# VectorE's queue in a differential-attention block: products of the next head moved behind the next minimum, and in grouped queries ahead of the exponential

## The reference

```python
def diff(qq, kk, vv, gate):                 # layer 0: 8 heads, 512 + 256 context tokens
    o1 = sweep_attention(qq[..., 0, :], kk[..., 0, :], vv)
    o2 = sweep_attention(qq[..., 1, :], kk[..., 1, :], vv)
    o = o1 - lam.astype(o1.dtype) * o2
    o = rms_norm(o, subln_g) * (1.0 - lam_init)
    return (o.reshape(...) * jax.nn.silu(gate)) @ w_out

q = rms_norm(q.reshape(B, L, GQ_HEADS, GQ_HEAD_DIM), qk_g[0])   # layer 1: 8 query heads, 2 key heads
k = rms_norm(k.reshape(B, L, GQ_KV_HEADS, GQ_HEAD_DIM), qk_g[1])
q, k = apply_rope(q, cos, sin), apply_rope(k, cos, sin)
o = sweep_attention(q, k_all, v_all)
y = (o.reshape(...) * jax.nn.silu(z)) @ w_out
```

## Time and profile before

| | |
|---|---|
| median of 3 runs | 1635.07 us (1634.91 to 1640.42) |
| the profiled execution | 1636.64 us, its span 1635.3 us |
| PE busy | 1533.2 us, 94% of the span |
| DVE, ACT, POOL busy | 69%, 38%, 43% |
| chain that ended last | PE 66%, DVE 15%, ACT 8%, POOL 5% |
| the heads' loops | about 845 to 1290 us, one every 55.0 us |
| grouped queries' 32 steps | about 1405 to 1590 us |

### The profile page before, as it was taken

The page is one execution under the profiler, slowest core; times in us unless marked ns, Lnnn a source line. Parts: engine busy times, 40 slices in busy tenths (PEclk is TensorE's granted clock), DMA queues, the critical chain, the costliest instruction groups (busy, mean ns, idle before and its releaser), DMA issues.

```text
span 1635.3 us, 22570 instructions
## 1 busy us (share of the span) xinstructions
PE 1533.2 (94%) x8093; PEld 1286.4 (79%) x8093; DVE 1133.5 (69%) x2396; ACT 624.7 (38%) x1560; POOL 710.1 (43%) x668
## 2 busy tenths in 40 slices
PE   5998989999999999999999999999997999899997
PEld 4787444788878887877798898889885787899886
DVE  7646766467777768737867777777777588777764
ACT  3313666232222220113453544554455355344431
POOL 6756000337667658685543044314425114523430
PEclk8997999999999999999999999999999999999999
DMA  6623000424444436653320011001102231111221
GB/s 185 196 77 103 1 1 1 140 68 148 129 139 126 129 105 208 203 192 106 122 66 27 26 52 53 26 27 52 53 25 80 107 112 52 53 52 39 65 91 52
DMA packets 115888, 142.62 MB, mean 87 GB/s; under 512 B 11048, under 2 KB 75200, under 8 KB 115776
## 3 DMA queue, kind: packets, MB, share of 16 engines
q1 hardware_dynamic: 89968, 91.77, 18.1%
q10 hardware_dynamic: 25808, 49.40, 9.1%
HBM read 132.74 MB, written 8.40 MB: 86 GB/s over the span
## 4 chain that ended last, share of the span: by engine, by line
PE 66%; DVE 15%; ACT 8%; POOL 5%; issue 4%; DMA 1%; ACTq 0%; SPq 0%; DVEq 0%; POOLq 0%
PE ps L502 17%; PE ps L504 17%; PE ps L503 17%; POOL w_lo L491 3%; PE ps L1445 2%; POOL w_hi L489 2%; PE ps L1249 2%; ACT p L2087 2%; PE ps L908 2%; DVE st L2864 2%; PE ps L889 2%; PE ps L941 1%; DVE p L2536 1%; ACT p L1713 1%; PE ps L1459 1%
## 5 line engine op out<-in xcount | busy, mean ns | idle before, releaser
L489 POOL TENSOR_SCALAR w_hi<-w_raw 128x512 fp32r<-128x512 f32 x308 | 236.1, 767 | 644.8 <-PE ps L504 488.1
L491 POOL TENSOR_TENSOR w_lo<-w_raw,w_hi 128x512 fp32r<-128x512 f32 x316 | 442.4, 1401 | 30.6 <-ACT w_hi L1635 4.9
L502 PE MATMUL ps<-w_hi,h_hi 128*128 128x384 f32 (+2 forms) x768 | 277.1, 361 | 8.2 <-POOL w_lo L491 2.9
L504 PE MATMUL ps<-w_hi,h_lo 128*128 128x384 f32 (+2 forms) x768 | 264.8, 345 | 0.0
L503 PE MATMUL ps<-w_lo,h_hi 128*128 128x384 f32 (+2 forms) x768 | 264.3, 344 | 0.0
L502 PE MATMUL ps<-h_hi,w_hi 128*128 128x512 f32 (+1 forms) x616 | 244.7, 397 | 6.5 <-POOL w_lo L491 2.6
L504 PE MATMUL ps<-h_hi,w_lo 128*128 128x512 f32 (+1 forms) x616 | 237.8, 386 | 0.0
L503 PE MATMUL ps<-h_lo,w_hi 128*128 128x512 f32 (+1 forms) x616 | 237.5, 385 | 0.0
L2582 DVE SCALAR_TENSOR_TENSOR mod_acc<-mod_piece,csil,mod_acc 128x512 f32<-128x512 f32 x140 | 156.7, 1159 | 22.2 <-DMA mod_piece<-in_ada_w 18.3
L502 PEld LDWEIGHTS ps<-w_hi,h_hi 128*128 128x128 f32 x768 | 146.1, 190 | 20.5 <-POOL w_lo L491 4.3
L503 PEld LDWEIGHTS ps<-w_lo,h_hi 128*128 128x128 f32 x768 | 146.5, 191 | 8.4 <-issue 0.5
(11 more groups left out here) (332 smaller groups left out, 3033.6 us busy)
## 6 DMA issues: line engine op xcount, KB each, us to landing
mod_piece<-in_ada_w ACTq DMA_DIRECT2D x96, 256.0 KB, 3.0
w_raw<-in_w_gate_up SPq DMA_DIRECT2D x88, 256.0 KB, 3.1
w_raw<-in_a_w_in SPq DMA_DIRECT2D x128, 128.0 KB, 2.2
w_raw<-in_w_down SPq DMA_DIRECT2D x22, 512.0 KB, 4.2
w_raw<-in_b_w_in SPq DMA_DIRECT2D x20, 512.0 KB, 3.6
w_raw<-in_w_out SPq DMA_DIRECT2D x16, 512.0 KB, 3.8
w_raw<-in_w_in SPq DMA_DIRECT2D x8, 512.0 KB, 3.9
w_raw<-in_w_o SPq DMA_DIRECT2D x8, 512.0 KB, 3.8
```

Of the source, the lines that this page charges most:

```text
L489: pool.tensor_scalar(hi[:, e, :], raw[:, e, :], 1.0, 0.0, ALU.mult, ALU.add).then_inc(*s["pool_step"].up())
L491: m = pool.tensor_tensor(lo[:, e, :], raw[:, e, :], hi[:, e, :], ALU.subtract)
L502: pe.matmul(out, a[0], b[0], start=start, stop=False)
L504: return pe.matmul(out, a[1], b[0], start=False, stop=stop)
```

## The change

In `dve_heads` the read-outs of a step's chunks are no longer issued at the end of that step but in the next step, behind its minimum, the first transposed part and the mix (steps 1 to 11 of heads 0 to 6), and what a loop leaves over (`held`) behind the minimum of the next head's first step. Before, they were issued in part before and in part behind the second L2885 of a step. PE and ACT keep their order there; head 7's own steps keep theirs on DVE too. In `act_grouped` the squares or tanh of a finished unit move from the end of the step to its start, and in `dve_grouped` the unit's rotation or z moves from behind the norm and the second L3092 to between the first L3092 and the norm. No instruction is added or removed.

```diff
@@ act_grouped
     for n in range(32):
+        unit = done_beside8(n)
+        if unit is not None:
+            act_read8(k, act, unit)
         if n > 0:
             act_copy8(k, act, n - 1, 0)
         act_exp8(k, act, n)
         if n > 0:
             act_copy8(k, act, n - 1, 1)
-        unit = done_beside8(n)
-        if unit is not None:
-            act_read8(k, act, unit)
@@ dve_heads
+    held = iter(())
     for hd in range(8):
         beside = dve_beside(k, dve, hd)
...
             if n == 11:
 
                 dve_head_mix(k, dve, hd, 5)
+            if n == 0:
+                for _ in held:
+                    pass
+            elif hd < 7:
+                fill(sum(HEAD_FILL[n - 1]) if n % 2 == 0 else HEAD_FILL[n - 1])
             if n == 3 and hd > 0:
                 dve_head_gate(k, dve, hd - 1)
             if n == 6 and hd > 0:
                 dve_head_y(k, dve, hd - 1)
-            if hd < 7:
-                fill(HEAD_FILL[n][0] if n % 2 else HEAD_FILL[n])
-            elif n in LAST_GATE_READ:
+            if hd == 7 and n in LAST_GATE_READ:
                 fill(KD)
             if late is not None and len(head_turns(late[1])) > 1:
                 dve_head_at(k, dve, *late, 1)
-            if n % 2 and hd < 7:
-                fill(sum(HEAD_FILL[n][1:]))
...
-        for _ in beside:
-            pass
+        held = beside
+    for _ in held:
+        pass
@@ dve_grouped
         if n > 0:
             dve_turned_lo8(k, dve, n - 1, 0)
+        unit = done_beside8(n)
+        if unit is not None:
+            dve_read8(k, dve, unit)
         dve_norm8(k, dve, n)
         if n > 0:
             dve_turned_lo8(k, dve, n - 1, 1)
-        unit = done_beside8(n)
-        if unit is not None:
-            dve_read8(k, dve, unit)
```

## The result

The changed kernel takes 1681.5 us (1679.13 to 1682.51, 4 runs) against 1635.92 for the kernel before on the same chip (1634.91 to 1640.42, 4 runs): 1.0272 times as long, with a 95% interval of 1.0255 to 1.0289. That is 45.6 us slower. The prediction had said 1663 us and a range to 1676: the direction was right, the size was not.

What follows compares the result with a forecast made beforehand. PE was taken as the bound (52.7 of 55 us a head loop). Net +3.5 us over seven loops gave +24, plus 1.5 for grouped queries and 3 for the clock: 1663 us expected, range 1645 to 1676.

Steps and rivals of the forecast that it cites:

- scores' waits of steps 6, 8, 9 go: Head loop: PE's scores no longer wait for ACT's exponential, as the minimum precedes the read-outs; 2.4 us a loop saved.
- POOL's and the transposed part's wait go: Head loop: PE's waits for split weights at chunk 7 (0.71 us) and a transposed part (0.33) were counted as saved.
- chunk 23's turn: Step 4 of a head loop: PE waits for DVE's late turned context tile, 0.8 us added.
- chunk 39's turn: Step 7 of a head loop: PE waits for v and rotation behind minimum and transposed part, 1.3 us added.
- scores of step 10: Head loop: step 9's minimum comes late behind DVE's queued work, so these scores wait about 0.6 us.
- chunk 57: Step 10 of a head loop: PE waits for z1's read-out, 1.4 us added.
- chunk 63's turn: Behind step 11's scores: PE waits for rotation after minimum, transposed part and mix, 2.8 us added.
- the clock: PE's clock falling behind long waits in the head loops; 3 us added to the total.
- The grouped part: Grouped queries: DVE's moved rotation delays norm and second low part; −3 to +4 us possible, +1.5 taken.
- The rival by which DVE would catch up in its idle time: Head loops: scores' waits go and read-outs fit, 1615 us; 5% for under −0.5%, 7% for within 0.5%.
- the third rival: Steps 10 or 11: PE reaches turns late anyhow, hiding up to 2.3 us a loop; +16, 1651 us; chance 16%.
- the second rival: Every head loop: the long wait at chunk 63 halves PE's clock, 1.85 us each, +13, 1673 us; chance 17%.

Runs made afterwards that it cites:

- the kernel held to step 9: Heads' read-outs held only for steps 0 to 9, later ones and grouped part as before the change; 1648.4 us, ratio 1.0084 to the kernel before.

## Why the prediction was wrong in size and right in kind

In one of the loops of 61.7 us, from the same pair of instructions before and after, in us:

| step of the prediction | predicted | measured |
|---|---|---|
| scores' waits of steps 6, 8, 9 go | −2.4 | −2.44 |
| POOL's and the transposed part's wait go | −1.04 | −0.99 |
| chunk 23's turn | +0.8 | +0.93 |
| chunk 39's turn | +1.3 | +1.46 |
| scores of step 10 | +0.6 | +0.70 |
| chunk 57 | +1.4 | +1.95 |
| chunk 63's turn | +2.8 | +3.75 |
| the clock | +0.4 | +1.31 |
| sum | +3.9 | +6.67 |

*What held.* Each of the four waits came at the instruction named, and each saving went as worked out. The method (from the start of the same step's scores, when PE wants a read-out and when DVE can have it) gave the terms that do not run beside POOL to within 0.16 us. The term of step 10 is right in size but not all at its place: 0.49 of the 0.70 us are waited at chunk 49, the first of tile 2's rows, for z0's read-out, a fifth late read-out that the walk through the 64 chunks took for one with room. It adds nothing, since step 10's scores start at 1007.21, 2.03 us behind the minimum of step 9 (1005.18), as the chain of the prediction has it; that it hides there is luck. The grouped part was rightly taken as next to nothing. The rival by which DVE would catch up in its idle time is refuted by the loop's 61.7 us, and the third rival, that PE would come late to the turns anyhow, by the same rows: PE did come late (DVE waited 3.74 us for step 11's scores), but DVE can't begin its chain before those scores, so the lateness hides nothing.

*What failed, first: the size of chunks 57 and 63.* The prediction took for the mix and the rotation the durations that they had at their old places, the stretched L2876 (1.25 us, at 944.06 and 950.93) included. It said of the stretch that it "falls there now and after" and left its size as it was. But a stretch is set by what is left of POOL's instruction at that moment: L2876 came to 1.91 and 1.92 us for 1.25, L2815 to 1.01 for 0.32, of which the rotation's last instruction gives back 0.41 (0.41 for 0.82). That is 0.55 us at chunk 57 and 0.95 at chunk 63, and the kernel without the splits shows it from the other side: their waits fall by 1.07 and 1.63, more than by the excess over the forecast, since the forecast had some stretch in it already. The loop in which L2876 met L489 as before waited 2.80 us at chunk 63, the very number of the forecast: so the sum was right for the stretch that it put in, and the stretch was wrong. The range of a stretch was to be had from the trace of before: its rows give the rule of the table above, by which an L2876 that meets an L491 at its start can take about 1.1 us more (1.29 less 0.2; a 256-wide one at 1243.29 took 1.47 us for 0.49), and the prediction put no such bound.

*Second: the clock.* It was the second rival, with 17% and a quarter of its price in the sum. It came in every loop: behind the waits of 3.73 to 3.75 us, but also behind the one of 2.80, and behind one of 2.96 in the kernel with the heads' part alone. So the clock would likely have fallen with the wait as forecast too (two waits near it, both with a fall), and the quarter was an error of its own. With 2.12 us it fell in three loops of six. The price of 1.85 us a fall was too high (1.31 by the scores' distance, 1.2 by the kernel with unneeded matmuls: 8.2 us in seven loops, 1.55 by the loops without splits), and near only by luck: the 5 us of the earlier trace rows end in the middle of a longer fall, whose next 5 us (730 to 735) are granted 0.68. Adding the two to the forecast, 7 × (0.95 + 0.55 + 0.9) = 17 us on 1663, gives 1680.

By the Trainium skill (SBUF — State Buffer, "Who interferes with whom") the order in which two contending instructions are issued, not their kind, decides which one stands blocked. The trace agrees: L2815, issued at 1021.97 while L491 runs, takes 1.01 us for 0.29 and L491 keeps its 1.26; L489, issued at 1020.17 while L2876 runs, takes 1.32 for 0.62.

What stays open: it was not tried to move POOL's splits away from the chains of chunks 57 and 63 with all of the work in place. Nor do the runs tell why the clock fell behind some waits of 2.12 us and not behind others.

## What to carry to other kernels

Taking work off the path of one consumer puts it on that of another: before an engine's order is changed, list for each moved item who wants it and when, counted from the event that now stands ahead of it, and move only those with room (here the read-outs of two steps of twelve and of the loop's end, for −0.7% where all together gave +2.7%). Where such a chain has instructions that another engine's can hold up, price them by what is left of that engine's instruction at their new place, not by what they took at the old one. And a saving in a loop is only one when the loop gets shorter: two of the partial orders here (step 7 alone, the end alone) took their wait away and found it at another one.

## What the runs showed of the hardware

- DVE's instructions with two inputs in SBUF stretch beside POOL's splits by up to 1.1 us each: L2876 (128x768) 1.02 us alone, 1.25 or 1.92 beside them; L2815 (128x128) 0.29 us alone, up to 1.27 beside them (steps 4, 7 and the end held, at 898.16), four times; L2816 (128x256) 0.41 alone, 1.54 at most (step 7 held, at 901.91). The shorter instruction loses relatively more.
- The size of a stretch is what is left of POOL's running instruction less 0.14 to 0.22 us.
- L2874 (128x768, one tensor read from SBUF, scaled by two numbers a partition) stretches as well: 0.68 us alone, 0.93 beside POOL in the kernel before (943.09), 1.39 with step 7 held (952.11). The read-outs from PSUM keep their times (0.28 and 0.42 us) in every row shown.
- POOL pays as well when it comes second: L489 (128x512) 0.62 us alone, 1.32 behind L2876.
- Waits of PE of 3.73 to 3.75 us were followed in every loop by a fall of the granted clock (0.64 for 3 us and 0.79 for the next 3 in the loop shown), and so were waits of 2.80 and 2.96 us; behind waits of 2.12 to 2.14 us (no splits) it fell in three loops of six; waits of 2.0 us in each loop (the kernel held to step 9) left it at 1.00. Unneeded matmuls in the long wait gained 8.2 us over the seven loops.
